# Moving 24 modulation rows into the projections, the first attention logits ahead of the recurrence's tail, and a wait behind the first recurrence units

## The reference, cut to what matters

```python
c_act = silu(c)
sh1, sc1, ga1, sh2, sc2, ga2 = split(c_act @ w_ada + b_ada, 6)        # 6 x 1024 values: the modulations
xn = rms_norm(h, g_mix) * (1 + sc1) + sh1
q, k, v, qi, ki, wi, xr, yr, gate_a, gate_b = split(xn @ w_in + b_in)
attn = dsa_attention(q, k, v, qi, ki, wi, rel_bias)                    # index scores pick 128 keys per query
rnn = rg_lru(causal_dwconv(xr), ...) * gelu(yr)
merged = sigmoid(gate_a) * (attn @ w_o_attn) + sigmoid(gate_b) * (rnn @ w_o_rnn)
h = h + ga1 * (merged @ w_out)
xn = rms_norm(h, g_ffn) * (1 + sc2) + sh2
h = h + ga2 * (feed-forward of xn)
```

## Time and profile before

| | |
|---|---|
| median of 3 runs | 1830.97 us (1829.56 to 1833.65) |
| the profiled execution | 1835.36 us, its span 1833.5 us |
| PE busy | 1771.9 us, 97% |
| DVE busy | 1069.5 us, 58% |
| POOL busy | 1470.9 us, 80% |
| ACT busy | 526.5 us, 29% |
| mean granted clock of PE | 0.983 of 2.4 GHz |

### The profile page before, as it was taken

One profiled execution on the slowest core, in us unless ns is written; L12 is line 12 of the kernel. 1 busy time (PEld: TensorE's weight loads), 2 busy tenths in 40 slices (PEclk: granted clock), 3 DMA queues, 4 the chain that ended last, 5 costly groups with the idle time before them and its releaser, 6 DMA issues.

```text
span 1833.5 us, 33590 instructions
## 1 busy us (share of the span) xinstructions
PE 1771.9 (97%) x11430; PEld 1567.8 (86%) x11430; DVE 1069.5 (58%) x1677; ACT 526.5 (29%) x775; POOL 1470.9 (80%) x2245
## 2 busy tenths in 40 slices
PE   4999998999999999999899999999999999999997
PEld 2767775577799999988799999999999999999886
DVE  6457897956767777722557656655764554555102
ACT  3245663320121111100434443443343211111001
POOL 1758995468999999999678867876885999999885
PEclk8899998999999999999999999999999999999999
DMA  8232223344423223233222212122222222222332
GB/s 322 89 127 95 93 89 113 133 155 149 148 95 92 92 92 92 92 103 103 69 76 76 81 70 81 70 71 80 81 70 70 92 92 95 99 92 92 104 103 92
DMA packets 55328, 184.42 MB, mean 101 GB/s; under 512 B 6673, under 2 KB 9905, under 8 KB 55250
## 3 DMA queue, kind: packets, MB, share of 16 engines
q1 hardware_dynamic: 49714, 169.14, 27.7%
q10 hardware_dynamic: 5536, 14.16, 2.3%
HBM read 178.56 MB, written 4.72 MB: 100 GB/s over the span
## 4 chain that ended last, share of the span: by engine, by line
PE 71%; POOL 15%; issue 9%; DMA 2%; SPq 1%; DVE 0%; ACT 0%; POOLq 0%; ACTq 0%; DVEq 0%
PE gp L392 22%; PE gp L393 22%; PE gp L394 22%; POOL Wlo L383 10%; POOL Whi L380 4%; POOL probe L379 2%; DMA raw<-units 2%; PE A L718 2%; DMA AW<-ada 1%; PE A L765 0%; PE A L714 0%; SPq L326 0%; PE A L767 0%; PE A L746 0%; PE A L758 0%
## 5 line engine op out<-in xcount | busy, mean ns | idle before, releaser
L383 POOL TENSOR_TENSOR Wlo<-raw,Whi 128x256 fp32r<-128x256 f32 x1120 | 973.8, 890 | 46.8
L392 PE MATMUL gp<-XNhi,Whi 128*128 128x264 f32 (+3 forms) x2736 | 850.2, 311 | 31.4 <-POOL Wlo L383 17.1
L393 PE MATMUL gp<-XNlo,Whi 128*128 128x264 f32 (+3 forms) x2736 | 839.0, 307 | 0.0
L394 PE MATMUL gp<-XNhi,Wlo 128*128 128x264 f32 (+3 forms) x2736 | 836.1, 306 | 0.0
L392 PEld LDWEIGHTS gp<-XNhi,Whi 128*128 128x128 f32 x2736 | 518.9, 190 | 68.6 <-POOL Wlo L383 18.3
L393 PEld LDWEIGHTS gp<-XNlo,Whi 128*128 128x128 f32 x2736 | 519.5, 190 | 24.9 <-issue 2.2
L394 PEld LDWEIGHTS gp<-XNhi,Wlo 128*128 128x128 f32 x2736 | 518.4, 189 | 23.7
L379 POOL TENSOR_TENSOR probe<-raw 1x1 f32<-1x1 f32 x560 | 177.0, 316 | 296.7 <-PE gp L394 253.5
L380 POOL TENSOR_SCALAR Whi<-raw 128x512 fp32r<-128x512 f32 x560 | 345.0, 616 | 0.0
L392 PE MATMUL gp<-AChi,Whi 128*128 128x512 f32 (+1 forms) x374 | 142.8, 382 | 0.0
L394 PE MATMUL gp<-AChi,Wlo 128*128 128x512 f32 (+1 forms) x374 | 142.6, 381 | 0.0
(11 more groups left out here) (314 smaller groups left out, 2273.8 us busy)
## 6 DMA issues: line engine op xcount, KB each, us to landing
raw<-units SPq DMA_DIRECT2D x280, 512.0 KB, 3.5
AW<-ada SPq DMA_DIRECT2D x16, 512.0 KB, 8.8
AWL<-ada SPq DMA_DIRECT2D x16, 512.0 KB, 4.6
AWL<-ada ACTq DMA_DIRECT2D x16, 512.0 KB, 4.1
bias_rows<-RB ACTq DMA_DIRECT2D x1, 2560.0 KB, 15.9
H<-xT SPq DMA_DIRECT2D x1, 2048.0 KB, 8.7
BIAS<-bias_rows ACTq DMA_DIRECT2D x1, 2048.0 KB, 9.2
out<-H SPq DMA_DIRECT2D x8, 256.0 KB, 2.2
```

Source lines behind the costliest of these rows:

```text
L383: ins = pool.tensor_tensor(lo[:, c:c + UNIT // 4], src[:, c:c + UNIT // 4], hi[:, c:c + UNIT // 4].bitcast(F32), ALU.subtract)
L392: pe.matmul(dst, Whi[s][:, k, :], rhi, start=start, stop=False)
L393: pe.matmul(dst, Whi[s][:, k, :], rlo, start=False, stop=False)
L394: return pe.matmul(dst, Wlo[s][:, k, :], rhi, start=False, stop=stop)
```

## The change

Rows 16 to 39 move into the projections and the first recurrence step, into the buffers `AW`: 16 before DVE's chain of tiny operations, two behind score 11, two behind score 17, four behind the first convolution. SP loads them behind units 1 to 9, in the numbers of `AHEAD`. The last 8 stay in the attention, one a step, now behind the step's logits. The merge and the residual have none, and ACT issues no row loads. PE's wait for the relus goes into the first `gates`, the wait for V into the first `values`. DVE takes the first two logits inside the last recurrence step, before the tail, the next two behind it, then the negations, two more, the first probabilities and the last two. The recurrence's tiles are laid out in another order. The functions `logits` and `probabilities` of DVE move up in the file unchanged.

```diff
+ADA_MID = 5 * KC
+AHEAD = [0, 4, 2, 2, 3, 3, 3, 3, 2, 2]
...
-                    XC0, GY0, RG, IG, DA, TH, M2, U1 = [sb(f"rnn_{n}", [P, S], frame=fr) for n in
-                                                      ("xc", "gelu", "r", "i", "a", "tanh", "mult2", "u")]
+                    XC0, GY0, IG, TH, RG, DA, M2, U1 = [sb(f"rnn_{n}", [P, S], frame=fr) for n in
+                                                      ("xc", "gelu", "i", "tanh", "r", "a", "mult2", "u")]
...
-            load_units(0, U_RNN)
+            def load_mid(c):
+                sp.wait_ge(ada_done, c + 1)
+                sp.dma_start(AW[c % ADA_SLOTS][:, :], ada[c, :, :]).then_inc(ada_in[c % ADA_SLOTS], 16)
+
+            for u in range(U_RNN):
+                load_unit(u)
+                for c in range(sum(AHEAD[:u]), sum(AHEAD[:u + 1])):
+                    load_mid(ADA_FIRST + c)
             sp.dma_start(CON[:, C_ONE:], consts[:, C_ONE:]).then_inc(con_in, 16)
             load_units(U_RNN, U_ROUT)
 
             def load_late(m):
-                sp.wait_ge(ada_done, ADA_SLOTS + ADA_FIRST + max(m - 1, 0))
-                sp.dma_start(AWL[m % 2][:, :], ada[ADA_FIRST + m, :, :]).then_inc(late_in[m % 2], 16)
+                sp.wait_ge(ada_done, ADA_SLOTS + ADA_MID + max(m - 1, 0))
+                sp.dma_start(AWL[m % 2][:, :], ada[ADA_MID + m, :, :]).then_inc(late_in[m % 2], 16)
...
             for j in range(KC):
                 load_unit(U_ROUT + 2 + j)
-                if j < KC - 1:
-                    load_late(2 * j + 2)
-                    load_late(2 * j + 3)
+                if j < KC - 2:
+                    load_late(j + 2)
...
-            pe.wait_ge(relu_done, NH * (QT - 1))
-
             def gates(b):
 
+                if b == 0:
+                    pe.wait_ge(relu_done, NH * (QT - 1))
...
             pe.wait_ge(proj_out, U_RNN + 2)
-            pe.wait_ge(v_ready, 1)
...
             def values(i, r, behind):
 
                 pe.wait_ge(p_ready, i * 2 + r + 1)
+                if i == 0 and r == 0:
+                    pe.wait_ge(v_ready, 1)
...
-            act.wait_ge(at_done, QT)
-            load_late(2 * KC)
-            load_late(2 * KC + 1)
...
-                load_late(2 * KC + 2 + 2 * t)
-                load_late(2 * KC + 3 + 2 * t)
-
-            norm_stats(1, lambda k: load_late(3 * KC + 2 + k) if k < KC - 2 else None)
+
+            norm_stats(1)
...
-                last_modulations(0, 0)
                 chunk(0, 0)
                 add(0, 1)
-                last_modulations(0, 1)
                 chunk(0, 1)
...
+            def modulate(m):
+                dve.wait_ge(late_in[m % 2], 16 + m // 2 * 16)
+                dve.tensor_tensor_reduce(AWL[m % 2][:, :], AWL[m % 2][:, :], CS[:, :], 1.0, 0.0, ALU.mult, ALU.add,
+                                         MOD[:, ADA_MID + m:ADA_MID + m + 1]).then_inc(ada_done, 1)
...
             dve.tensor_tensor(LAM[:, 4, :], l1, LAM[:, 2, :], ALU.subtract).then_inc(lb_max, 1)
+            modulation(ADA_FIRST, ADA_FIRST + 16)
...
+                if n in (11, 17):
+                    c = ADA_FIRST + 16 + (0 if n == 11 else 2)
+                    modulation(c, c + 2)
...
                     ins.then_inc(xc_ready, 1)
+                if b == 0:
+                    modulation(ADA_MID - 4, ADA_MID)
...
                     take((1, 2, 3))
+                    if b == KC:
+                        dve.wait_ge(bias_in, 16)
+                        logits(0, 0, 0)
                     dve.wait_ge(mult_ready, b)
...
+            logits(0, 0, 1)
             for i in range(1, QT):
                 dve.tensor_scalar(NEG[i][:, :], SC[i][:, :], TAKEN, MASKED, ALU.not_equal, ALU.mult)
-
-            dve.drain()
-            dve.wait_ge(bias_in, 16)
+            dve.drain()
+            logits(0, 1, 0)
+            probabilities(0, 0)
+            logits(0, 1, 1)
             dve.wait_ge(rgate_ready, KC)
...
-            for r in range(2):
-                logits(0, r, 0)
-                logits(0, r, 1)
-            probabilities(0, 0)
             for i in range(QT):
                 for r in range(2):
-                    for s in range(2):
-                        modulate(i * 2 + r, s, mod_column(i * 2 + r, s))
...
                     if i + 1 < QT:
                         logits(i + 1, r, 1)
+                    if r == 0:
+                        modulate(i * 2)
...
                                   AThi[:, :, i * P:(i + 1) * P].bitcast(F32), ALU.subtract).then_inc(at_done, 1)
+                modulate(i * 2 + 1)
...
             for t in range(4):
-                for q in range(2):
-                    modulate(t + KC, q, mod_column(t + KC, q))
```

More of the change, by code:

```diff
@@ L335, in load_units, with load_unit @@
                         sp.dma_start(raw[s][:, :], units[bass.ds(i * RAW + s, 1), :, :]).then_inc(raw_in[s], 16)
-            load_units(0, U_RNN)
+            def load_unit(u):
+                sp.wait_ge(weights_ready, u + 1)
+                sp.dma_start(raw[u % RAW][:, :], units[u, :, :]).then_inc(raw_in[u % RAW], 16)
+            def load_mid(c):
[5 more added lines that the diff above has]
+                    load_mid(ADA_FIRST + c)
             sp.dma_start(CON[:, C_ONE:], consts[:, C_ONE:]).then_inc(con_in, 16)
@@ L341, in load_late @@
             def load_late(m):
-                sp.wait_ge(ada_done, ADA_SLOTS + ADA_FIRST + max(m - 1, 0))
-                sp.dma_start(AWL[m % 2][:, :], ada[ADA_FIRST + m, :, :]).then_inc(late_in[m % 2], 16)
-            def load_unit(u):
-                sp.wait_ge(weights_ready, u + 1)
-                sp.dma_start(raw[u % RAW][:, :], units[u, :, :]).then_inc(raw_in[u % RAW], 16)
+                sp.wait_ge(ada_done, ADA_SLOTS + ADA_MID + max(m - 1, 0))
+                sp.dma_start(AWL[m % 2][:, :], ada[ADA_MID + m, :, :]).then_inc(late_in[m % 2], 16)
             load_late(0)
@@ L1222, in add @@
                     dve.drain()
-                def last_modulations(i, c):
-                    if m == 1:
-                        modulate(i + (KC + 4), c, mod_column(i + (KC + 4), c))
-                last_modulations(0, 0)
                 chunk(0, 0)
                 add(0, 1)
-                last_modulations(0, 1)
                 chunk(0, 1)
@@ L1235, in residual @@
                         add(i, c)
-                        last_modulations(i, c)
                         chunk(i, c)
@@ L1441, in gated @@
+            logits(0, 0, 1)
+            for i in range(1, QT):
+                dve.tensor_scalar(NEG[i][:, :], SC[i][:, :], TAKEN, MASKED, ALU.not_equal, ALU.mult)
+            dve.drain()
+            logits(0, 1, 0)
+            probabilities(0, 0)
+            logits(0, 1, 1)
+            dve.wait_ge(rgate_ready, KC)
             def gated(j):
```

75 lines of the change are left out of this document (31 added, 44 removed).

## The result

The changed kernel takes 1821.3 us (median of 4 runs, 1819.95 to 1822.78) against 1831.1 us (1829.56 to 1833.65): the ratio is 0.9935, with a 95% interval from 0.9923 to 0.9948. By these medians it is 9.8 us faster (their own ratio is 0.9947, and the ratio on record with its interval stands for 9.5 to 14.1 us). I had forecast 1809 in a range of 1798 to 1822: right in sign, with about half the gain, and 0.7 us inside the very end of the range. The profiled execution after took 1822.29 us; its span is 13.1 us shorter than the one before (1833.5), where the sum had said 22.2.

The account below looks back on a forecast made before the run. PE was busy 97% of the span, so only its waits and low-clock stretches could shrink. The terms summed to -22.2 us, from 1835.4 to 1813.2; with the median 4.4 lower, the forecast was 1809 us, range 1798 to 1822.

Parts of the forecast that it names:

- Term 1: After the last scores: PE's relu wait moves to the first recurrence unit's gates, -2.8 us, bounds -2.8 and 0.
- rival B: At the gates: another wait replaces the moved relu wait, which then gains 0; 1812 us, chance 0.08.
- Term 2: Projections: the twenty-four rows moved there cost +4 us, bounds 0 and +16.
- the covered case: Projections: the lower bound for the moved rows, 0 us, with all their cost covered.
- rival C: Projections: rows slow POOL, loads and rows come later, the softplus chain starves; +6.6 us, 1838 us, chance 0.04.
- Term 3: From recurrence to attention: first logits ahead of the recurrence's tail gain -6 us, bounds -2 and -8.
- Term 4: Attention: eight rows instead of sixteen gain -6.5 us in PE's waits and clock, bounds -3 and -8.
- Terms 5 and 6: No rows in the merge, -6.4 us (bounds -3, -6.7), nor in the projection behind, -4.5 us (bounds -2, -5).
- rival A: Handover, attention, merge and projection behind: only part of the gains comes, -8.8 us in all; 1822 us, chance 0.2.
- best bounds: Whole kernel: every term at its most favourable bound, together given as -33.3 us, 1798 us.

Follow-up runs that it names:

- e1: The kernel before with only the scores' wait for the relus moved to the first gates; 1831.1 us, ratio 0.9989 against the kernel before.
- e3: The changed kernel without modulation rows 16 to 39, their columns set to a constant; 1809.1 us, ratio 0.9867 against the kernel before.
- e11: The changed kernel with the three mask operations behind the first head block's last logits; 1821.1 us, ratio 0.9940 against the kernel before.
- e2: The kernel before with only the new logits' order, tile layout and V's wait moved, rows in old places; 1828.2 us, ratio 0.9981.
- e9: The changed kernel without its 8 rows in the attention, their columns constant; 1821.9 us, ratio 0.9941 against the kernel before.
- e5: The changed kernel with the modulation vector copied to PSUM for the first sixteen rows; 1814.2 us, ratio 0.9904 against the kernel before.
- e4: The changed kernel with 11 rows ahead of the chain, 2 and 3 among scores, 8 in the first recurrence step; 1817.5 us, ratio 0.9916.

## Why the prediction was right and wrong, step by step

*Term 1, -2.8.* Right: -2.9 alone in e1, and in the changed kernel one unit took 9.11 us instead of 12.00. That the scores came 12 us late did not matter, since PE was as late; rival B asked for a delay against PE, and there was none.

*Term 2, +4: the step that failed.* It cost 11.8 us (e3): 3.4 in waits for POOL, 7.8 at the second score batch, 0.6 in the recurrence. Four things were off. (1) POOL's half unit under rows: at most 4.2 us in my sum, 4.1 to 5.1 in the trace. I took the 2.73 of the earlier trace rows, where one row met two subtractions; back to back nearly every subtraction meets one, and four of the five probes as well. I had left the probe at its undisturbed time. POOL fell back further than its cover, and PE waited 3.4 us (by the unit ends) where I had 1. (2) The last row ended at 87.9, not 85, since the row loads stood behind unit loads that waited for the slower POOL: DVE waited 5.5 us at 78.9. (3) The constants, which I had landing near 99, before DVE wants them, landed at 106.8. The chain I moved as a block, and it took 20.0 us instead of 16.4, as its tiny operations met POOL, which now had backlog and no pause. Either alone would have made the weights 10.7 or 11.7 us late instead of 5 (e11 shows the constants as the later of the two). No run moved the constants' load alone, so how much of the 7.8 us an earlier load would give back is open. PE's wait at the second batch was 4.8 us instead of 3. (4) To that wait I gave no clock: 7.2 us at 0.53 cost 3.4. The places are the ones named (the load groups, the chain, the batch), the upper bound of +16 held, and the value I took in it was too near the covered case.

The loop of rival C (POOL slowed by rows, unit loads and so rows late, chain late) is what happened, at a quarter of its strength: 8 us of delay and not 30.

*How long row and subtraction hold each other up.* A subtraction beside rows took 1.63 us in the mean and a row 1.73 to 1.78. The rule of the Trainium skill, SBUF — State Buffer, section "SBUF: two separate sides", that the port pair is an exclusive lock held for a whole instruction, gives by my estimate 1.22 + 0.72 = 1.94 for each. The trace is 0.2 to 0.3 below it, but the direction is right, and the one-element probe at 1.17 us, about the 1.22 of an undisturbed row, is what a lock would do. In the prediction I weighed the rule by a price of 1.5 us; followed through the probe and the chain's operations too, it would have come nearer.

*Term 3, -6.* The stretch lost 5.2 us in e2 and wherever the clock held, 3.8 in the first execution. The new wait of "about 2 us" behind pair 2 is there with 2.67. Mis-sized by the tail: I took its four microseconds from the time before, and it took 5.6 (296.6 to 302.2), the scan alone 1.63 beside POOL where it had taken 1.22.

*Term 4, -6.5.* Near in size (-7.5, of which up to 1.8 may be the clock, by e2) and right in reason: PE's waits gone, clock 1.00, and e9 shows PE's own work as the new bound.

*Terms 5 and 6, -6.4 and -4.5.* -5.9 and -5.1, -11.0 together against -10.9 forecast. Right, with e2's doubt on 1.4 us of it.

The time lies on rival A's number (1822), but not by its way: A wanted terms 3 to 6 more than halved. They gave 22.3 of 23.4, term 3 as in the first trace, and 7.8 of the 9.1 us that are missing in the span are term 2's. The sum of the profiled spans, 13.1 us, is also above the medians' 9.8: the execution before that was profiled was 4.3 us slower than its median, the one after 1.0. That the time fell inside the range at all is luck: its upper end lay 0.7 us above.

*The bounds and the signs.* The sum of the best bounds counts term 1 twice: it is -30.5, not -33.3, so 1800.5 and not 1798. Of the signs that I named, PE's start of unit 10, the attention, the merge and the projection came as said; the chain started at 87.8, just outside 83 to 87, and the first transposes came 3.5 us nearer, not 6. The sign for term 2, PE waits for POOL of over 5 us in 65 to 100, did not show (2.3 in the waits, 3.4 by the unit ends), although term 2 was the cause. The greater part came by way of the index weights, where I had named no sign with a size.

## What to carry to other kernels

Before work moves into an engine's idle time, take the neighbour's durations from a stretch where both are busy without a break, for every operation, the smallest included, and follow every load that queues behind the slower neighbour, not only those of the moved work: here the constants' load came 10.7 us late. If the work is one vector against many tiles, put the vector in PSUM: that alone took 6 to 7 us of the 11.8 back. Fill an idle stretch only up to the point at which something else would have ended it (here ACT's exponentials at 80 us), and place a remainder in several small gaps, not in one: with 8 rows in the recurrence's first step it took 5.2 us more than with 4.

## What the runs showed of the hardware that I had not expected

An operation on one element (POOL's probe) took 1.17 us instead of 0.18 beside rows with two SBUF inputs, and operations on 128 x 8 values on DVE, with one input or two, took 0.48 to 0.76 us instead of 0.15 to 0.20 beside POOL's splitting. The clock fell inside a score batch drawn out to 5 us, with PE busy 4.5 of them by the profile but 13 matmuls in place of 23 (e5), and held through one drawn out to 3.6 us (e4); the same 2.67 us wait in the handover was followed by a clock of 0.72 in one execution and of 1.00 in another of the same kernel. So a clock loss behind a wait of that size can be forecast as a chance, not as a sum.
